# A weight block's low part on GpSimd: four subtractions of 256 columns for one of 1024

## What is computed

```python
for layer in range(2):
    shift_m, scale_m, gate_m, shift_f, scale_f, gate_f = adaln_modulation(c, *ada[layer])
    h = rmsnorm(x, pre_m) * (1.0 + scale_m) + shift_m
    x = x + gate_m * rmsnorm(mixers[layer](h), post_m)      # SSD + MLA, then GLA + NSA
    h = rmsnorm(x, pre_f) * (1.0 + scale_f) + shift_f
    x = x + gate_f * rmsnorm(swiglu(h, *ffns[layer]), post_f)
...
q, k, v, gu, gv, gate_a, gate_b = jnp.split(rmsnorm_2(x, norm_mix_g[l]) @ w_in[l], splits, axis=-1)
merged = sigmoid(gate_a) * (moba_attention(q, k, v) @ moba_w_proj[l]) + sigmoid(gate_b) * (
    gmlp_spatial_gating(gu, gv, ...) @ gmlp_w_proj[l])
x = x + merged @ w_out[l]
x = x + memory_cross_attention(rmsnorm_2(x, norm_xa_g[l]), rmsnorm_2(mem, norm_mem_g[l]), ...)
x = x + peer_ffn(rmsnorm_2(x, norm_ffn_g[l]), ...)
return rmsnorm_2(x, final_g)
```

## Time and profile before

| | us |
|---|---|
| median of three runs | 2167.47 |
| profiled execution | 2166.55 |
| its span, first to last instruction | 2164.4 |
| TensorE busy (91%) | 1961.8 |
| VectorE busy (64%) | 1384.9 |
| ScalarE busy (45%) | 979.8 |
| GpSimd busy (30%), all of it before 1393 us | 653.3 |
| of this the 247 low parts of line 1261 | 621.0 |

### The profile page before, as it was taken

The page is one execution under the profiler, slowest core; times in us unless marked ns, Lnnn a source line. Parts: engine busy times, 40 slices in busy tenths (PEclk is TensorE's granted clock), DMA queues, the critical chain, the costliest instruction groups (busy, mean ns, idle before and its releaser), DMA issues.

```text
span 2164.4 us, 33504 instructions
## 1 busy us (share of the span) xinstructions
PE 1961.8 (91%) x13340; PEld 1807.4 (84%) x13340; DVE 1384.9 (64%) x2380; ACT 979.8 (45%) x1415; POOL 653.3 (30%) x285
## 2 busy tenths in 40 slices
PE   6778889995969778999989889899999999999998
PEld 5776689995967657998888789899998888999997
DVE  5787765546892677333733334998887888666665
ACT  5334454444433334444544544556664333444444
POOL 2451534444641423433865646500000000000000
PEclk9889989997989889999999999999999999999999
DMA  7552456663545324554543334457776676565443
GB/s 294 187 171 92 147 185 235 248 227 110 185 145 214 118 78 155 189 184 173 180 138 136 122 112 156 139 183 220 211 215 239 252 256 243 204 234 195 184 179 124
DMA packets 94234, 392.82 MB, mean 181 GB/s; under 512 B 7648, under 2 KB 41584, under 8 KB 55552
## 3 DMA queue, kind: packets, MB, share of 16 engines
q1 hardware_dynamic: 94080, 390.69, 51.3%
HBM read 372.83 MB, written 15.73 MB: 180 GB/s over the span
## 4 chain that ended last, share of the span: by engine, by line
PE 69%; DVE 16%; ACT 3%; POOL 3%; issue 2%; DMA 0%; DVEq 0%; ACTq 0%; SPq 0%; POOLq 0%
PE ps L559 9%; PE ps L561 9%; PE ps L560 9%; PE acc L555 8%; PE acc L556 7%; PE acc L557 7%; DVE arena L1290 3%; POOL wlo L1261 3%; PE acc L559 2%; PE acc L560 2%; PE acc L561 2%; DVE arena L1441 2%; DVE arena L1763 2%; PE acc L1216 1%; PE ps L1216 1%
## 5 line engine op out<-in xcount | busy, mean ns | idle before, releaser
L2236 ACT ACTIVATE whi<-raw 128x1024 fp32r<-128x1024 f32 x559 | 589.7, 1059 | 543.5 <-PE acc L557 273.5
L1261 POOL TENSOR_TENSOR wlo<-raw,whi 128x1024 fp32r<-128x1024 f32 x247 | 621.0, 2526 | 687.0 <-ACT whi L2236 686.1
L559 PE MATMUL ps<-hhi,whi 128*128 128x256 f32 x1880 | 545.0, 290 | 31.0 <-POOL wlo L1261 13.6
L560 PE MATMUL ps<-hlo,whi 128*128 128x256 f32 x1880 | 539.2, 287 | 0.0
L561 PE MATMUL ps<-hhi,wlo 128*128 128x256 f32 x1880 | 539.0, 287 | 0.0
L1261 DVE TENSOR_TENSOR wlo<-raw,whi 128x1024 fp32r<-128x1024 f32 x312 | 389.5, 1249 | 230.9 <-ACT whi L2236 230.9
L559 PEld LDWEIGHTS ps<-hhi,whi 128*128 128x128 f32 x1880 | 368.6, 196 | 37.7 <-issue 16.4
L560 PEld LDWEIGHTS ps<-hlo,whi 128*128 128x128 f32 x1880 | 368.5, 196 | 2.9
L561 PEld LDWEIGHTS ps<-hhi,wlo 128*128 128x128 f32 x1880 | 367.9, 196 | 0.0
L555 PE MATMUL acc<-whi,chi 128*128 128x512 f32 x752 | 296.7, 395 | 4.6 <-POOL wlo L1261 3.0
L556 PE MATMUL acc<-whi,clo 128*128 128x512 f32 x752 | 295.3, 393 | 0.0
(11 more groups left out here) (448 smaller groups left out, 2567.5 us busy)
## 6 DMA issues: line engine op xcount, KB each, us to landing
raw<-in_peer_down SPq DMA_DIRECT2D x64, 1024.0 KB, 5.0
raw<-in_peer_up SPq DMA_DIRECT2D x64, 1024.0 KB, 5.3
arena<-in_ada SPq DMA_DIRECT2D x80, 512.0 KB, 4.2
raw<-in_w_gate SPq DMA_DIRECT2D x22, 1024.0 KB, 4.8
raw<-in_w_up SPq DMA_DIRECT2D x22, 1024.0 KB, 4.9
raw<-in_w_down SPq DMA_DIRECT2D x22, 1024.0 KB, 4.8
arena<-spill SPq DMA_DIRECT2D x14, 1024.0 KB, 7.1
spill<-hT_t SPq DMA_DIRECT2D x22, 448.0 KB, 6.2
```

The source lines that it names most:

```text
L559: e.matmul(out, hi, xh, start=start, stop=False, skip_group_check=True)
L560: e.matmul(out, hi, xl, start=False, stop=False, skip_group_check=True)
L1261: e.tensor_tensor(out=lo, in0=w, in1=hi.bitcast(F32), op=ALU.subtract).then_inc(*X(("lo", j)))
L2236: e.activation(hi, w, ACT.Copy, scale=1.0).then_inc(*self.A(("hi", j)))
```

## The change

`cut_lo` makes a loop of its one subtraction. On GpSimd the step is 256 columns, so that a block takes four operations on neighbouring column ranges; on VectorE the step is the whole width, as before. The wait for the high part stands once ahead of the loop. Each of the four counts up GpSimd's semaphore, and only the last carries the block's key `("lo", j)`, for which TensorE and the DMA queue wait.

```diff
             if self.W.lo_engine(j) == who:
                 w, hi, lo, _ = self.W.parts(j)
                 e.wait_ge(*self.at("hi", j))
-                e.tensor_tensor(out=lo, in0=w, in1=hi.bitcast(F32), op=ALU.subtract).then_inc(*X(("lo", j)))
+                n = w.shape[1]
+                step = 256 if who == "G" else n
+                for c in range(0, n, step):
+                    sl = slice(c, c + step)
+                    e.tensor_tensor(out=lo[:, sl], in0=w[:, sl], in1=hi[:, sl].bitcast(F32), op=ALU.subtract).then_inc(
+                        *X(*([("lo", j)] if c + step >= n else [])))
```

## The result

The changed kernel takes 2154.58 us (median of 4 runs, 2153.11 to 2160.08) against 2167.1 for the kernel before (4 runs, 2165.3 to 2170.33): ratio 0.9945, 95% interval 0.9923 to 0.9967. It is faster by 12.5 us, 0.55%. The forecast was 2141: the sign is right, the gain is half of what was told. The profiled execution took 2160.08 us (span 2158.3), the longest of the four; its shares and waits are these. Lines behind the changed loop have moved by five: L1290 is now L1295, L1441 is L1446, L1763 is L1768, L1904 is L1909, L2778 is L2783; L1261 is L1265.

What follows compares the result with a forecast made beforehand. TensorE was taken as the bound, busy 1961.8 of 2164.4 us, leaving some 202 us to win. Terms -25 - 12 - 11 + 15 + 4.5 + 2.5 = -26 us from 2166.55 gave 2140.5, stated as 2141; range 2106 to 2182.

Steps and rivals of the forecast that it cites:

- Turns go by the instruction: GpSimd and VectorE alternate one instruction each, so VectorE enters between quarters; a stalled VectorE operation becomes 1.65 us shorter.
- Rival 1: VectorE gets no turn inside a block, so its stalls stay and grow by 0.38: about 2190 us; chance 0.08.
- (a): TensorE's 7 waits on VectorE's adaLN accumulation L1290, 41.7 us, of which 60% would go: -25 us.
- (b): TensorE's four waits on VectorE's softmax scaling L1441, 13.6 us, and shorter ones behind them: -12 us.
- (c): Waits booked elsewhere that start with a stalled VectorE operation (L803, three L1975, three more places): -11 us together.
- (d): TensorE's waits on GpSimd's low parts L1261, 20 and two short ones, at +0.7 each: +15 us.
- (f): An activation's low half (L2778) three times behind a block in GpSimd's queue, and one load: 4 x 0.6 = +2.5 us.
- (e): From 1050 to 1090 us, VectorE's 12 operations of 1024 columns delay GpSimd's last block 4 to 8 us: +4.5 taken.
- The other signs: Expected: GpSimd busy some 750 us, VectorE about 14% of chain, L1290's maximum near 1.3 us, L1261 waits some 45.
- rival 2: VectorE enters every gap of blocks TensorE waits for; 22 x 2.0 = +44, gains halved: some 2195 us; chance 0.12.
- are covered: From 300 to 480 us, a block's extra 0.4 to 2.0 us cost nothing, GpSimd being busy only 78.80 us.
- without that cover: If GpSimd's idle time from 300 to 480 us hid nothing, 31 blocks x 0.4 would cost 12 us.

Runs made afterwards that it cites:

- Experiment 9: The changed kernel with GpSimd's blocks whole in both feed-forward stages and from w_mqk until VectorE's 1024-column string has ended: 2117.75 us, ratio 0.9776.
- Experiments 5: The changed kernel with GpSimd's feed-forward blocks cut only once, after column 256 (256 + 768): 2133.3 us.
- experiment 6: The changed kernel with GpSimd's feed-forward blocks cut only once, after column 768 (768 + 256): 2142.0 us.
- experiments 1: The changed kernel with GpSimd's blocks of w_gate, w_up and w_down (both feed-forward stages) left whole: 2131.0 us, ratio 0.983.
- 4: The changed kernel with VectorE's own low parts in the two feed-forward stages also made in quarters: 2138.3 us, ratio 0.9866.
- 7: The changed kernel with GpSimd's blocks whole in both feed-forward stages and for w_gu, w_gmv and w_mv: 2129.2 us, ratio 0.9813.
- 3: The changed kernel with all of GpSimd's low parts in two operations of 512 columns instead of four of 256: 2134.9 us, ratio 0.985.
- 8: The changed kernel with feed-forward blocks whole and each later quarter waiting by semaphore for the end of the one before: 2148.5 us.

## Why the prediction was half right

**Turns go by the instruction (held).** The base of the forecast was that VectorE gets in between two quarters, though none of them has a wait. L1768's 1.17 us, L1446's 0.90 at most and L1295's 1.21 at most beside quarters show it. Rival 1, the four as one, is the exception, once in the whole run.

**(a) Waits on L1290: -25 forecast, -31.7 measured** (41.7 to 10.0). **(b) Waits on L1441: -12, and -6.7 measured** (13.6 to 6.9); the operations did become short, but four times TensorE still waits for the string around them. **(c) Other places: -11 was too much.** L803's wait went from 4.9 to 4.3, not by 2. The four L1975 (now L1980) have a median of 0.91 us instead of 2.51, but their starts span 10.3 us instead of 12.1, a gain of 1.8 and not 3.3. **(d) More waiting for low parts: +15 at 22 places.** All waits on them are 60.6 us after and 28.8 before, short ones included. With the feed-forward stages (4.2 and 10.7 us) and the string's stage (5.5 + 4.8 + 2.3 us, before 5.8) taken out, 33 us are left against 23: +10. **(f) L2778: +2.5, and +4.5 measured** (waits of 14.3 us in all before, 18.8 after).

Together, (a) to (d) and (f) said -30.5 us for the stages with mixers. TensorE's idle time there fell by 31 us in one profile and 28 in the other, which leaves some -7 for (c) and all that has no term, by subtraction. So the mechanism held here; that the sum came out so close is luck in part, since (a) and (d) turned out better than told and (b), (c) and (f) worse. These stages gained 39 and 44 us all the same, because TensorE was also busy 8 and 16 us less. The text had left its clock outside the sum ("the gain side of the range is a little longer").

**(e) The string from 1050: +4.5 forecast, +11.5 measured.** The mechanism stood in the text, and so did the price: three blocks in its 20 us are the 6.7 us of a block that were measured. GpSimd's 16 blocks came 7.4 us late, inside the "4 to 8" of which the sum took the low end; the other 4.2 us are TensorE's busy time at the lower clock, for which the sum had no term. That one operation would wait for 27 quarters was not foreseen. Experiment 9 gets the 10 us back by leaving these blocks whole.

**The other signs.** GpSimd has its 988 operations, but 830.7 us busy and not 750, as the turns of VectorE lie in them. VectorE's share of the chain is 14%, as told. L1290's maximum is 2.28 us, not 1.3: the two longest met GpSimd's uncut product (L2812), and beside quarters it is 1.21, as told. Its median rose from 0.75 to 1.04: more of its operations meet a quarter, each for less. The string of 592.27 went from 7.11 us to some 4.5. The waits on L1261 came to 58.3 us in the rows, past the 45 that were told and short of rival 2's 70.

**The step that failed is "are covered".** The text took GpSimd's 78.80 busy us of 180 as cover for the first feed-forward stage and put it at nothing; the second, from 833 to 1018 us, it did not price at all. They cost 5.7 and 15.3 us, 21 together, where forecast and result lie 14 apart. What made up for a part of this was the 8 us and more that TensorE's busy time gave in the stages with mixers. A busy share is no cover. Each of GpSimd's blocks there waits for ScalarE's high part, and the high part of the block in question comes behind VectorE's product and the activation's split in ScalarE's list, so GpSimd sits idle 5.5 us and still can't begin sooner. The cover of a block is the time from its end to TensorE's need: 0.43 us, in one block of each iteration. It could have been read before: the rows at 879.08 and 880.81 show a 1024-column VectorE operation asking 1.73 us into a block of 2.40, and four quarters have a gap at 2.1. Rival 2 described just this ("VectorE goes in at every gap of just those blocks that TensorE waits for") but counted only the 22 places where TensorE waited already; stages that are full, 180.00 us of 180 and 184.80 of 184.80, have none in that list, and there the loss fell. Even the price named "without that cover", 12 us, used the fixed 0.4 and not a turn.

The Trainium skill, SBUF — State Buffer, section "Who interferes with whom", says that the shared pair is an exclusive lock held for the whole instruction, and that issue order decides who blocks. Experiments 5 and 6 agree: the same two instructions in the other order move the second feed-forward stage by 7.8 us. The L1909 of 19.28 us does not: it asked before 27 quarters began, and all of them went ahead of it.

## What to carry to other kernels

When two engines take turns by the instruction, cutting one engine's work is a priority given to the other: it pays where the other's result is waited for, and costs where its own is, so choose the size by stage and keep whole the blocks that the bound engine needs next. A helper's idle time is no slack if it is waiting for its own input; measure from the end of each block to the moment it is needed, in the fullest stage above all, since that stage shows no waits before the change. And look where in the block the other engine asks: a cut before that moment was free here, one after it was not.

## What the runs showed of the hardware

A run of GpSimd instructions without a wait can keep VectorE out. In the changed kernel L1909 asked at 1041.31 us, 0.03 before a quarter began, and got in only after 27 of them, 19.28 us instead of 1.22. It came again in its second profile (19.24 us) and in experiments 1, 4 and 5 (19.3 each), each time through 27 quarters (in the second profile the first of them had just begun), after which it got in without a pause of GpSimd. In 7 it took 12.84 us, through ten quarters and two whole blocks, up to a pause. It did not come where the pieces had 512 columns (3) or where a semaphore wait parted them (8), one case each. Nor did it come in experiment 6, where the quarters follow without a wait and the operation asked just as in the changed kernel, 0.03 us before a quarter began: it got in behind that one. So neither the gapless run nor the moment of asking, as far as a trace can tell it, is enough. Nearly all other VectorE operations that met quarters got in after the one in progress: in the changed kernel one GpSimd operation, held up in its turn, began during 425 operations of VectorE, two began during two, and 27 during one. The Trainium skill, GPSIMD Engine Reference, section "Instruction dispatch", has a core begin the next instruction when its own share of one is done, with no barrier between. That fits a case that needs gapless GpSimd instructions, but not that VectorE gets in everywhere else. What decides between the two is open. In the changed kernel the event itself seems to cost little (without it, in experiment 6, the stage takes 108.8 us, no less); in 7 it cost TensorE a wait of 10.4 us.

A GpSimd subtraction had a fixed part of about 0.13 us: 0.70 for 256 columns and 2.42 for 1024, so 3 x 0.13 a block, the +0.38 of the forecast; the piece of 768 with one of 256 takes 2.54.
